# Stationary weights read with a step of two columns, and activations at another distance from the weights

## The chip, the cores and the metric

The kernel runs on one core of a Trainium2 chip. A core has a matrix engine (TensorE, PE in the rows; its weight loads are shown apart as PEld), VectorE (DVE), ScalarE (ACT), GpSimd (POOL) and SyncE (SP), which here only starts DMA transfers. All share an on-chip memory of 128 partitions (SBUF); TensorE writes to PSUM. The metric is the time of one execution on the device in microseconds (us), as the median over several runs. Before the change it is 2870.81 us over three runs (2864.52 to 2885.74).

## The reference

A transformer-like stack over 256 tokens of width 1024, batch 1, in float32. Six stages of the first block (two layers: feed-forward, a four-branch mixer, feed-forward) are followed by four layers of a second block (a mixer, cross-attention on a memory of 256 tokens, feed-forward). Nearly all the arithmetic is in products of the activations with weight matrices:

```
def _swiglu(x, w_gate, w_up, w_down):
    return (jax.nn.silu(x @ w_gate) * (x @ w_up)) @ w_down
...
for l in range(DEPTH):                                   # 2 layers
    x = x + 0.5 * _swiglu(_rmsnorm(x, ffn1_norm[l]), ffn1_w_gate[l], ffn1_w_up[l], ffn1_w_down[l])
    z = _rmsnorm(x, mix_norm[l]) @ w_in[l]               # 1024 x 6660, split over four branches
    ...                                                  # convolutions, two attentions
    x = x + merged @ w_out[l]
    x = x + 0.5 * _swiglu(_rmsnorm(x, ffn2_norm[l]), ffn2_w_gate[l], ffn2_w_up[l], ffn2_w_down[l])
for i in range(DEPTH_2):                                 # 4 layers
    x = x + mix                                          # diff_attention, hgrn2 or chunked_sgu
    x = x + mem_cross_attention(rmsnorm(x, norm_cross[i]), mem_n, ca_w_q[i], ca_w_kv[i], ca_w_o[i])
    x = x + swiglu(rmsnorm(x, norm_ffn[i]), ffn_w_gu[i], ffn_w_down[i])
return rmsnorm(x, norm_final)
```

D_FF is 2816 in both blocks.

## The kernel before

**Weight units.** The host cuts every weight matrix into units of 128 partitions x 2048 columns (1 MB). A column unit (`column_unit`) holds 256 output columns of a matrix with 1024 rows: eight blocks (k = 0 to 7) of 256 columns each. A row unit (`row_unit`) holds 256 rows of a matrix with 1024 columns: two blocks (kt) of 1024. `weight_units` lists some 460 of them in the order of use. They pass through a ring of five slots. SP starts the transfer of a unit into slot j of `raw` once TensorE has finished the unit that was there (semaphore `unit_done`, line 385). ScalarE copies it, rounded to float32r, into `wh` (`high`, line 1113), and GpSimd writes the remainder raw - wh, as float32r, into `wl` (`low`, line 400). `wl` lies on the same addresses as `raw`. TensorE waits for `low_ready`.

**Products.** Activations are split the same way into a high and a low part: ah and al, mh and ml, gh and gl (the gated values of the feed-forward stages), oh and ol, and others. `product` (lines 451 to 457) makes each block's product from three float32r matmuls, all accumulated into the same 256 columns of PSUM:

```
pe.matmul(out, sl, vh, ...)      # line 454
pe.matmul(out, sh, vl, ...)      # line 455
pe.matmul(out, sh, vh, ...)      # line 456
```

The second argument is stationary (128 columns, loaded into the array) and the third moves (256 columns). A unit is 16 such triples, 48 matmuls. In `features`, `features_by_input`, the two row-unit loops of `ffn` and the branch outputs of the mixer, the stationary operand is a run of 128 neighbouring columns of `wh` or `wl` (`wcut`), and activations move. In `tokens` and `tokens_by_input`, 128 tokens of the activations are stationary and 256 weight columns move. One unit of the four-branch mixer is used both ways: its first 128 columns by `features(..., fcs=1)`, and then by `tokens`.

**Order.** Every engine runs its own list of instructions in program order, and semaphores tie the lists together. Nothing is reordered by a scheduler.

**Addresses.** `sb` hands out SBUF space one tensor after another. `raw`/`wl` and `wh` (40,960 bytes per partition each) begin at 0 modulo 256, counted from `raw`. After `x` a gap of 192 bytes is left (line 147), so that ah, al, full, mh, ml, the parameters and constants begin at 192 modulo 256. A second gap (line 162) puts the work area with gh, gl, oh, ol and the rest at 192 too. Slots, blocks and halves of a block are multiples of 512 bytes apart. So in every product matmul the first byte of the activations is 192 behind the first byte of the weights, modulo 256. The constant matrices `decays` and the tensors lh and ll, which are multiplied with each other at lines 934 and 935, both begin at 192.

Of the kernel before, what the change touches and what calls it, by code (L numbers as in the profile page):

```python
# [25 lines left out]
P = 128  # L26
T = 256
TB = T // P
D = 1024
KD = D // P  # L30
DFF = 2816
FP = DFF // 256
UW = 2048
# [95 lines left out]
def build(nc, w_units, params_d, consts_d, hot_d, rel_d, x_d, mem_d, ws_d, bs_d, out_d,  # L129
          table_d, units=UNITS, stop_after=None):  # L130

    at = [nc.sbuf_base]
# [9 lines left out]
    raw_at = at[0]  # L142
    raw = sb("raw", RING * UW)
    wl = sb("wl", RING * UW, F32R, offset=at[0] - 4 * RING * UW)
    wh = sb("wh", RING * UW, F32R)
    x = sb("x", KD * T)
    at[0] += 192
    acts_at = at[0]
    ah = sb("ah", KD * T, F32R)
    al = sb("al", KD * T, F32R)  # L150
# [8 lines left out]
    root = sb("root", 4 * T + 8)  # L159
    rr = root[:, 3 * T:4 * T + 2]  # L160
    small = sb("small", 136)
    at[0] += (raw_at + 192 - at[0]) % 256
    work_at = at[0]
    WORK = 12288
    work = sb("work", WORK)
# [197 lines left out]
    with nc.Block() as block:  # L363
# [49 lines left out]
        def _(pe):  # L413
# [34 lines left out]
            def wcut(t, j, first, width):  # L448
                return t[:, j * UW + first:j * UW + first + width]

            def product(out, parts, start, stop, **kw):

                for k, (sh, sl, vh, vl) in enumerate(parts):
                    pe.matmul(out, sl, vh, start=start and k == 0, stop=False, **kw)  # L454
                    pe.matmul(out, sh, vl, start=False, stop=False, **kw)  # L455
                    ins = pe.matmul(out, sh, vh, start=False, stop=stop and k == len(parts) - 1, **kw)  # L456
                return ins

            def features(out, j, xh, xl, fcs=2, col=256, halfway=None):

                for fc in range(fcs):
                    if fc and halfway is not None:
                        halfway()
                    for k in range(KD):
                        parts = [(wcut(wh, j, k * 256 + fc * P, P), wcut(wl, j, k * 256 + fc * P, P),
                                  xh[:, k * T:(k + 1) * T], xl[:, k * T:(k + 1) * T])]
                        ins = product(out[:, fc * col:fc * col + T], parts, k == 0, k == KD - 1)
                return ins

            def features_by_input(out, j, xh, xl, acts, pieces=False):  # L470

                for k in range(KD):
                    if k % 2 == 0:
                        pe.wait_ge(acts, c.next(acts))
                    if k % 2 == 0 and pieces:
                        pe.wait_ge(*((low_ready, 1) if k == KD - 2 else (first_low_ready, k // 2 + 1)))
                    for fc in range(2):
                        parts = [(wcut(wh, j, k * 256 + fc * P, P), wcut(wl, j, k * 256 + fc * P, P),
                                  xh[:, k * T:(k + 1) * T], xl[:, k * T:(k + 1) * T])]
                        ins = product(out[:, fc * 256:fc * 256 + T], parts, k == 0 and fc == 0, k == KD - 1,  # L480
                                      skip_group_check=True)
                return ins
# [92 lines left out]
            def ffn(memory=False):  # L575
# [50 lines left out]
                def down(j, u, n, src, first, last):  # L626
                    pe.wait_ge(gated_ready, u + (r0 + 1))
                    pe.wait_ge(low_ready, n + 1)
                    for kt in range(2):
                        for dc in range(KD):  # L630
                            out = y[dc // 4][:, (dc % 4) * T:(dc % 4 + 1) * T]
                            parts = [(wcut(wh, j, kt * D + dc * P, P), wcut(wl, j, kt * D + dc * P, P),
                                      gh[:, src + kt * T:src + kt * T + T],
                                      gl[:, src + kt * T:src + kt * T + T])]
                            ins = product(out, parts, first and kt == 0 and dc % 2 == 0,
                                          last and kt == 1, skip_group_check=True)
                    ins.then_inc(unit_done, 1)
# [6 lines left out]
                for pair in range(KD // 2):  # L644
                    for u in (FP - 2, FP - 1):
                        j = (n1 + u) % RING
                        for dc in (2 * pair, 2 * pair + 1):
                            out = y[dc // 4][:, (dc % 4) * T:(dc % 4 + 1) * T]
                            parts = [(wcut(wh, j, kt * D + dc * P, P), wcut(wl, j, kt * D + dc * P, P),
                                      gh[:, u * 512 + kt * T:u * 512 + (kt + 1) * T],  # L650
                                      gl[:, u * 512 + kt * T:u * 512 + (kt + 1) * T]) for kt in range(2)]
                            ins = product(out, parts, False, u == FP - 1, skip_group_check=True)
                        if pair == KD // 2 - 1:
                            ins.then_inc(unit_done, 1)
                    if pair < KD // 2 - 1:
                        ins.then_inc(columns_done, 1)
# [59 lines left out]
            def mix1(l):  # L716
# [14 lines left out]
                keys, both = g_bank(copied), g_bank(copied)  # L731
                pe.wait_ge(low_ready, unit[0] + 1)
                j = unit[0] % RING
                features(keys, j, ah, al, fcs=1)
                tokens(both, j, ah, al).then_inc(unit_done, 1)
                unit[0] += 1
                projection(2, copied, ah, al)
# [2 lines left out]
                def branch_part(k):  # L740

                    b = BRANCHES[k // 5]
                    if PARTS[k % 5] == "gate":
                        projection(1, gate_used, ah, al)
                        return
                    outs = [s_bank(copied), s_bank(copied)]
                    for n in (2, 1):
                        also[sbank[0] - n] = (half_copied, c.next(half_copied))
                    pe.wait_ge(low_ready, unit[0] + 1)
                    j = unit[0] % RING  # L750
                    pe.wait_ge(acts_ready, c.next(acts_ready))
                    for dc in range(KD):
                        parts = [(wcut(wh, j, kt * D + dc * P, P), wcut(wl, j, kt * D + dc * P, P),
                                  bh[:, (2 * b + kt) * T:(2 * b + kt + 1) * T],
                                  bl[:, (2 * b + kt) * T:(2 * b + kt + 1) * T]) for kt in range(2)]
                        ins = product(outs[dc // 4][:, (dc % 4) * T:(dc % 4 + 1) * T], parts, True, True)
                    ins.then_inc(unit_done, 1)
                    unit[0] += 1
# [2011 lines left out]

def column_unit(a):

    return a.reshape(KD, P, 256).transpose(1, 0, 2).reshape(P, UW)


def row_unit(a):

    return a.reshape(2, P, D).transpose(1, 0, 2).reshape(P, UW)  # L2780


def columns_of(a):
    return [column_unit(a[:, n:n + 256]) for n in range(0, a.shape[1], 256)]


# [7 lines left out]
def weight_units(v):  # L2794
    out = []
    for l in range(L1):
        out += ffn_units(v["ffn1_w_gate"][l], v["ffn1_w_up"][l], v["ffn1_w_down"][l])
        win = v["w_in"][l]

        out += columns_of(win[:, 0:1280])  # L2800
        q = win[:, 1280:1536].reshape(D, 4, HD)[:, [0, 2, 1, 3]].reshape(D, 256)
        out += [column_unit(q)] + columns_of(win[:, 1536:2560])
        gates = win[:, 2564:]
        for b in BRANCHES:
            own = columns_of(gates[:, b * D:(b + 1) * D])
            name = ("conf_w_out", "sc_w_out", "swa_w_o", "fox_w_o")[b]
            out += own[0:2] + [row_unit(v[name][l])] + own[2:4]
        out += columns_of(v["w_out"][l])
        out += ffn_units(v["ffn2_w_gate"][l], v["ffn2_w_up"][l], v["ffn2_w_down"][l])
    for i, kind in enumerate(MIXERS):  # L2810
        kv = columns_of(v["ca_w_kv_2"][i])
        if kind == "diff":
            a = columns_of(v["da_w_in_2"][i // 3])
            out += [a[n] for n in (0, 4, 8, 9, 1, 5, 10, 11, 2, 6, 3, 7)] + kv[0:4]
            out += columns_of(v["da_w_out_2"][i // 3])
        elif kind == "hgrn":
            a = v["hg_w_in_2"][i // 3]
            out += (columns_of(a[:, D:2 * D]) + columns_of(a[:, 0:D]) + columns_of(a[:, 2 * D:]) + kv[0:4]
                    + columns_of(v["hg_w_out_2"][i // 3]))
        else:  # L2820
            a = v["sg_w_in_2"][i // 3]
            out += columns_of(a[:, D:]) + columns_of(a[:, 0:D]) + kv[0:4] + columns_of(v["sg_w_out_2"][i // 3])
        out += columns_of(v["ca_w_q_2"][i]) + kv[4:8] + columns_of(v["ca_w_o_2"][i])
        out += ffn_units(v["ffn_w_gu_2"][i][:, :DFF], v["ffn_w_gu_2"][i][:, DFF:], v["ffn_w_down_2"][i])
    assert len(out) == UNITS
    return np.stack(out)
# [74 lines left out]
```

## Time and profile before

| | |
|---|---|
| median of three runs | 2870.81 us |
| the profiled execution's own span | 2878.8 us |
| TensorE busy, matmuls | 2822.3 us (98%), 24,180 matmuls |
| TensorE busy, weight loads | 2771.7 us (96%) |
| GpSimd busy | 2108.9 us (73%) |
| ScalarE busy | 1333.4 us (46%) |
| VectorE busy | 1066.5 us (37%) |
| granted TensorE clock, mean | 0.989 |
| memory traffic | 496.88 MB, mean 173 GB/s |

The profile is of one execution. A matmul's record overlaps the next one's, since matmuls are pipelined and their ends are modelled: a record of about 280 ns does not mean that a matmul costs that much. What one costs in a stream is the distance from its start to the next one's start. In the groups of instructions, "G<-ah,wl 128\*128 128x256" names the output, then the moving operand, then the stationary one; 128x256 is the moving operand's shape.

### The profile page before, as it was taken

To read this page: it belongs to the slowest core of one execution; us is meant where nothing else is said; L and a number is where in the kernel's file an instruction comes from. 1 tells how busy PE (TensorE), PEld (TensorE's weight loads), DVE (VectorE), ACT (ScalarE), POOL (GpSimd) and SP (SyncE) were. 2 spreads that over 40 slices of the span, in tenths; PEclk is the share of its full clock that TensorE was granted. 3 is DMA by queue.
4 is the path that set the end of the run, shared out by engine and by line. 5 is a ranking of instruction groups with operands and counts; after the bars stand their busy time and mean duration, and the time that the engine had idled before them with its cause. 6 is when DMAs were issued, how large, how long until landed. Compare 5 with 4: busy or idle time off the path is not lost.

```text
span 2878.8 us, 55910 instructions
## 1 busy us (share of the span) xinstructions
PE 2822.3 (98%) x24180; PEld 2771.7 (96%) x24180; DVE 1066.5 (37%) x1865; ACT 1333.4 (46%) x1490; POOL 2108.9 (73%) x462
## 2 busy tenths in 40 slices
PE   8999999999999999999999999999999999999998
PEld 8999889999999899999999998999999999999998
DVE  4217534213155443445333144333123331453331
ACT  5335544344355454345443484444354443454442
POOL 6777657878876578776768783659886688767785
PEclk9999999999999899999999999999999999999999
DMA  7974344555554355554445542445554455544553
GB/s 231 193 198 170 135 144 176 191 185 188 199 184 152 112 192 189 182 185 147 168 169 191 191 177 87 158 144 197 191 204 153 147 195 196 191 147 161 176 192 116
DMA packets 74197, 496.88 MB, mean 173 GB/s; under 512 B 8399, under 2 KB 13135, under 8 KB 14968
## 3 DMA queue, kind: packets, MB, share of 16 engines
q1 hardware_dynamic: 68344, 485.88, 46.9%
q10 hardware_dynamic: 5632, 7.62, 2.7%
q8 instruction: 191, 3.13, 0.4%
q14 instruction: 30, 0.25, 0.0%
HBM read 490.05 MB, written 3.41 MB: 171 GB/s over the span
## 4 chain that ended last, share of the span: by engine, by line
PE 86%; POOL 4%; DMA 3%; issue 3%; DVE 2%; ACT 2%; ACTq 0%; SPq 0%; POOLq 0%; DVEq 0%
PE G L454 21%; PE G L456 21%; PE G L455 21%; PE S L454 5%; PE S L456 5%; PE S L455 5%; POOL wl L400 4%; DMA raw<-w_units 2%; PE G L691 1%; PE S L1042 1%; ACT wh L1113 1%; DMA bias<-tables 0%; PE S L842 0%; PE S L799 0%; PE S L805 0%
## 5 line engine op out<-in xcount | busy, mean ns | idle before, releaser
L400 POOL TENSOR_TENSOR wl<-raw,wh 128x2048 fp32r<-128x2048 f32 x458 | 2108.7, 4616 | 740.5 <-ACT wh L1113 719.0
L1113 ACT ACTIVATE wh<-raw 128x2048 fp32r<-128x2048 f32 x456 | 873.7, 1918 | 1045.6 <-DMA raw<-w_units 1045.5
L454 PE MATMUL G<-ah,wl 128*128 128x256 f32 x4304 | 1209.2, 281 | 15.6 <-DVE wl L1768 8.9
L455 PE MATMUL G<-al,wh 128*128 128x256 f32 x4304 | 1200.6, 279 | 0.0
L456 PE MATMUL G<-ah,wh 128*128 128x256 f32 x4304 | 1200.3, 279 | 0.0
L454 PEld LDWEIGHTS G<-ah,wl 128*128 128x128 f32 x4304 | 816.4, 190 | 24.1 <-issue 15.1
L455 PEld LDWEIGHTS G<-al,wh 128*128 128x128 f32 x4304 | 815.2, 189 | 0.6
L456 PEld LDWEIGHTS G<-ah,wh 128*128 128x128 f32 x4304 | 814.1, 189 | 0.0
L454 PE MATMUL S<-gh,wl 128*128 128x256 f32 x1408 | 391.4, 278 | 3.4 <-POOL wl L400 3.4
L455 PE MATMUL S<-gl,wh 128*128 128x256 f32 x1408 | 391.3, 278 | 0.0
L456 PE MATMUL S<-gh,wh 128*128 128x256 f32 x1408 | 391.2, 278 | 0.0
L454 PEld LDWEIGHTS S<-gh,wl 128*128 128x128 f32 x1408 | 265.0, 188 | 3.7 <-issue 3.7
L456 PEld LDWEIGHTS S<-gh,wh 128*128 128x128 f32 x1408 | 265.1, 188 | 0.0
L455 PEld LDWEIGHTS S<-gl,wh 128*128 128x128 f32 x1408 | 265.1, 188 | 0.0
L1921 DVE TENSOR_TENSOR G<-G,root 128x512 f32<-128x512 f32 x88 | 61.5, 698 | 361.3 <-PE G L456 361.3
L1959 DVE SCALAR_TENSOR_TENSOR S<-S,x 128x512 f32<-128x512 f32 x28 | 19.6, 700 | 367.1 <-PE S L456 365.9
L1919 DVE TENSOR_TENSOR G<-G,root 128x512 f32<-128x512 f32 x88 | 61.4, 698 | 184.4 <-PE G L456 184.1
L454 PE MATMUL G<-mh,wl 128*128 128x256 f32 x384 | 108.3, 282 | 3.3 <-DVE ml L2120 2.8
L454 PE MATMUL G<-wh,al 128*128 128x256 f32 x384 | 108.0, 281 | 0.8 <-DVE ll L2563 0.8
L455 PE MATMUL G<-wl,ah 128*128 128x256 f32 x384 | 107.2, 279 | 0.0
L456 PE MATMUL G<-wh,ah 128*128 128x256 f32 x384 | 107.1, 279 | 0.0
L456 PE MATMUL G<-mh,wh 128*128 128x256 f32 x384 | 106.9, 279 | 0.0
(371 smaller groups left out, 3786.3 us busy)
## 6 DMA issues: line engine op xcount, KB each, us to landing
raw<-w_units SPq DMA_DIRECT2D x459, 1024.0 KB, 4.8
bias<-tables ACTq DMA_DIRECT2D x24, 128.0 KB, 3.2
tables<-trow ACTq DMA_DIRECT2D x12, 192.0 KB, 9.0
con<-consts SPq DMA_DIRECT2D x1, 1056.0 KB, 16.8
x<-x_in SPq DMA_DIRECT2D x4, 256.0 KB, 5.8
raw<-w_units SPq DMA_DIRECT2D x4, 256.0 KB, 6.9
memx<-mem_in ACTq DMA_DIRECT2D x1, 1024.0 KB, 7.4
out<-full SPq DMA_DIRECT2D x4, 256.0 KB, 2.5
```

What stands on the lines that cost most here:

```text
L400: pool.tensor_tensor(wl[:, j * UW:(j + 1) * UW], raw[:, j * UW:(j + 1) * UW], wh[:, j * UW:(j + 1) * UW].bitcast(F32), ALU.subtract)\
L454: pe.matmul(out, sl, vh, start=start and k == 0, stop=False, **kw)
L455: pe.matmul(out, sh, vl, start=False, stop=False, **kw)
L456: ins = pe.matmul(out, sh, vh, start=False, stop=stop and k == len(parts) - 1, **kw)
L691: ins = pe.matmul(out, v_of(kc), pt[:, kc * 512 + n * P:kc * 512 + (n + 1) * P], start=kc == 0, stop=kc == nk // P - 1)
L1042: ins = pe.matmul(out[:, h * T:(h + 1) * T], qf[:, f * T + g * P:f * T + (g + 1) * P], kc[:, f * T:(f + 1) * T], start=dc == 0, stop=dc == 1)
L1113: act.activation(wh[:, j * UW:(j + 1) * UW], raw[:, j * UW:(j + 1) * UW], ACT.Copy)\
L1919: dve.tensor_tensor(pairs(gate), pairs(gate), along, ALU.mult).then_inc(scaled, 1)
L1921: dve.tensor_tensor(pairs(value), pairs(value), along, ALU.mult).then_inc(up_scaled, 1)
L1959: dve.scalar_tensor_tensor(xs if last else held[k], held[k], factor, xs, ALU.mult, ALU.add)\
```

## The change

It has two parts. First, wherever weights are stationary, the 128 columns of a load are every other column of a run of 256 (`every_other`: the even ones for the first half of the outputs, the odd ones for the second). The host interleaves the two halves of every 256 columns beforehand (`interleaved`), so that the same numbers reach the same outputs. Units whose weights move (`token_columns_of`) are left in the old order, and so is the unit that is used both ways, whose 128 columns are still read with a step of one (`first_features`). Second, both gaps are 96 bytes instead of 192: activations, constants and work area begin 96 behind the weights modulo 256. `decays` and lh still begin at the same place modulo 256.

```diff
@@ addresses @@
-    at[0] += 192
+    at[0] += 96
     acts_at = at[0]
...
-    at[0] += (raw_at + 192 - at[0]) % 256
+    at[0] += (raw_at + 96 - at[0]) % 256
@@ TensorE @@
+            def every_other(j, first, odd):
+
+                return tuple(wcut(t, j, first, 2 * P).rearrange("p (i f) -> p f i", f=2)[:, odd, :] for t in (wh, wl))
...
-            def features(out, j, xh, xl, fcs=2, col=256, halfway=None):
-
-                for fc in range(fcs):
+            def features(out, j, xh, xl, halfway=None):
+
+                for fc in range(2):
                     if fc and halfway is not None:
                         halfway()
                     for k in range(KD):
-                        parts = [(wcut(wh, j, k * 256 + fc * P, P), wcut(wl, j, k * 256 + fc * P, P),
-                                  xh[:, k * T:(k + 1) * T], xl[:, k * T:(k + 1) * T])]
-                        ins = product(out[:, fc * col:fc * col + T], parts, k == 0, k == KD - 1)
+                        parts = [(*every_other(j, k * 256, fc), xh[:, k * T:(k + 1) * T], xl[:, k * T:(k + 1) * T])]
+                        ins = product(out[:, fc * 256:fc * 256 + T], parts, k == 0, k == KD - 1)
                 return ins
+
+            def first_features(out, j, xh, xl):
+
+                for k in range(KD):
+                    parts = [(wcut(wh, j, k * 256, P), wcut(wl, j, k * 256, P),
+                              xh[:, k * T:(k + 1) * T], xl[:, k * T:(k + 1) * T])]
+                    product(out[:, 0:T], parts, k == 0, k == KD - 1)
...
@@ row units: both loops of ffn, and the mixer's branch outputs @@
-                            parts = [(wcut(wh, j, kt * D + dc * P, P), wcut(wl, j, kt * D + dc * P, P),
+                            parts = [(*every_other(j, kt * D + dc // 2 * 256, dc % 2),
@@ host @@
+def interleaved(a):
+
+    return a.reshape(a.shape[0], -1, 2, P).transpose(0, 1, 3, 2).reshape(a.shape)
...
 def row_unit(a):
 
-    return a.reshape(2, P, D).transpose(1, 0, 2).reshape(P, UW)
+    return interleaved(a).reshape(2, P, D).transpose(1, 0, 2).reshape(P, UW)
 
 
 def columns_of(a):
+    return [column_unit(interleaved(a[:, n:n + 256])) for n in range(0, a.shape[1], 256)]
+
+
+def token_columns_of(a):
     return [column_unit(a[:, n:n + 256]) for n in range(0, a.shape[1], 256)]
```

`features_by_input` is edited as `features` is. The order of the instructions on every engine and their waits are the same before and after; only source lines are numbered differently.

## Rows read from the trace of the kernel before

**Rows 1.** The page's busy times with instruction counts; the core's span and clock.
```profile
PE 2822.3 (98%) x24180; PEld 2771.7 (96%) x24180; DVE 1066.5 (37%) x1865; ACT 1333.4 (46%) x1490; POOL 2108.9 (73%) x462
...
core 0: 2878.8 us, clock 0.989
```

**Rows 2.** TensorE's groups by form, line 454: count | busy us, mean ns | idle before.
```profile
L454 PE MATMUL G<-ah,wl 128*128 128x256 f32 x4304 | 1209.2, 281 | 15.6 <-DVE wl L1768 8.9 <-DVE wl L1800 3.4 <-DVE merged L2178 3.2
...
L454 PE MATMUL S<-gh,wl 128*128 128x256 f32 x1408 | 391.4, 278 | 3.4 <-POOL wl L400 3.4
...
L454 PE MATMUL G<-mh,wl 128*128 128x256 f32 x384 | 108.3, 282 | 3.3 <-DVE ml L2120 2.8 <-DVE logf L2655 0.5
L454 PE MATMUL G<-wh,al 128*128 128x256 f32 x384 | 108.0, 281 | 0.8 <-DVE ll L2563 0.8
...
L454 PE MATMUL G<-oh,wl 128*128 128x256 f32 x384 | 106.5, 277 | 0.0
...
L454 PE MATMUL G<-wh,ml 128*128 128x256 f32 x256 | 72.2, 282 | 0.0
...
L454 PE MATMUL S<-mh,wl 128*128 128x256 f32 x128 | 35.9, 280 | 1.5 <-issue 1.5
...
L454 PE MATMUL G<-soh,wl 128*128 128x256 f32 x64 | 19.5, 304 | 4.2 <-ACT kc L1238 4.2
...
L454 PE MATMUL G<-hoh,wl 128*128 128x256 f32 x64 | 17.8, 278 | 0.0
```

**Rows 3.** TensorE by stretch: window, its us, busy (matmuls), clock, DMA share, GB/s.
```profile
42.00:177.00 135.00, 135.00 (x1148) 1.00 0.91 202
467.00:641.00 174.00, 174.00 (x1480) 1.00 0.51 181
655.00:827.00 172.00, 172.00 (x1520) 1.00 0.54 192
...
1148.00:1254.00 106.00, 106.00 (x903) 1.00 0.52 184
1486.00:1653.00 167.00, 167.00 (x1476) 1.00 0.54 193
...
1942.00:2114.00 172.00, 172.00 (x1520) 1.00 0.55 197
2308.00:2473.00 165.00, 165.00 (x1458) 1.00 0.54 192
2704.00:2864.00 160.00, 160.00 (x1414) 1.00 0.48 171
```

**Rows 4.** Matmuls of 128 moving columns: timeline, chain (start, us), and group by form.
```profile
1354.58 1.47 PE L702 MATMUL G<-con,full 128*128 128x128 f32 x12
...
1438.83 7.15 PE G L691 x64
...
L702 PE MATMUL G<-con,full 128*128 128x128 f32 x48 | 6.2, 272 | 0.0
```

**Rows 5.** Timeline of TensorE (start, us): `decays` products, and first and last of twenty token matmuls.
```profile
1733.85 0.28 PE L454 MATMUL G<-wh,al 128*128 128x256 f32 x1
...
1736.09 0.28 PE L455 MATMUL G<-wl,ah 128*128 128x256 f32 x1
...
1743.76 0.28 PE L935 MATMUL S<-decays,ll 128*128 128x256 f32 x1
...
1744.48 0.28 PE L935 MATMUL S<-decays,ll 128*128 128x256 f32 x1
```

**Rows 6.** The chain that ended last: shares of the span by engine and line.
```profile
PE 86%; POOL 4%; DMA 3%; issue 3%; DVE 2%; ACT 2%; ACTq 0%; SPq 0%; POOLq 0%; DVEq 0%
PE G L454 21%; PE G L456 21%; PE G L455 21%; PE S L454 5%; PE S L456 5%; PE S L455 5%; POOL wl L400 4%; DMA raw<-w_units 2%; PE G L691 1%; PE S L1042 1%; ACT wh L1113 1%; DMA bias<-tables 0%; PE S L842 0%; PE S L799 0%; PE S L805 0%
```

**Rows 7.** The low split's group (count | busy, mean ns | idle before), and the weights' transfers.
```profile
L400 POOL TENSOR_TENSOR wl<-raw,wh 128x2048 fp32r<-128x2048 f32 x458 | 2108.7, 4616 | 740.5 <-ACT wh L1113 719.0
...
raw<-w_units SPq DMA_DIRECT2D x459, 1024.0 KB, 4.8
```

More of the change, by code:

```diff
@@ L477, in features_by_input @@
                     for fc in range(2):
-                        parts = [(wcut(wh, j, k * 256 + fc * P, P), wcut(wl, j, k * 256 + fc * P, P),
-                                  xh[:, k * T:(k + 1) * T], xl[:, k * T:(k + 1) * T])]
+                        parts = [(*every_other(j, k * 256, fc), xh[:, k * T:(k + 1) * T], xl[:, k * T:(k + 1) * T])]
                         ins = product(out[:, fc * 256:fc * 256 + T], parts, k == 0 and fc == 0, k == KD - 1,
@@ L648, in ffn @@
                             out = y[dc // 4][:, (dc % 4) * T:(dc % 4 + 1) * T]
-                            parts = [(wcut(wh, j, kt * D + dc * P, P), wcut(wl, j, kt * D + dc * P, P),
+                            parts = [(*every_other(j, kt * D + dc // 2 * 256, dc % 2),
                                       gh[:, u * 512 + kt * T:u * 512 + (kt + 1) * T],
@@ L733, in mix1 @@
                 j = unit[0] % RING
-                features(keys, j, ah, al, fcs=1)
+                first_features(keys, j, ah, al)
                 tokens(both, j, ah, al).then_inc(unit_done, 1)
@@ L752, in branch_part @@
                     for dc in range(KD):
-                        parts = [(wcut(wh, j, kt * D + dc * P, P), wcut(wl, j, kt * D + dc * P, P),
+                        parts = [(*every_other(j, kt * D + dc // 2 * 256, dc % 2),
                                   bh[:, (2 * b + kt) * T:(2 * b + kt + 1) * T],
@@ L2801, in weight_units @@
         q = win[:, 1280:1536].reshape(D, 4, HD)[:, [0, 2, 1, 3]].reshape(D, 256)
-        out += [column_unit(q)] + columns_of(win[:, 1536:2560])
+        out += [column_unit(interleaved(q))] + token_columns_of(win[:, 1536:1792])
+        out += columns_of(win[:, 1792:2304]) + token_columns_of(win[:, 2304:2560])
         gates = win[:, 2564:]
@@ L2810, in weight_units @@
     for i, kind in enumerate(MIXERS):
-        kv = columns_of(v["ca_w_kv_2"][i])
+        keys, values = v["ca_w_kv_2"][i][:, 0:D], v["ca_w_kv_2"][i][:, D:]
+        kv = columns_of(keys) + token_columns_of(values)
         if kind == "diff":
-            a = columns_of(v["da_w_in_2"][i // 3])
+            a = v["da_w_in_2"][i // 3]
+            a = columns_of(a[:, 0:2 * D]) + token_columns_of(a[:, 2 * D:])
             out += [a[n] for n in (0, 4, 8, 9, 1, 5, 10, 11, 2, 6, 3, 7)] + kv[0:4]
@@ L2817, in weight_units @@
             a = v["hg_w_in_2"][i // 3]
-            out += (columns_of(a[:, D:2 * D]) + columns_of(a[:, 0:D]) + columns_of(a[:, 2 * D:]) + kv[0:4]
+            out += (columns_of(a[:, D:2 * D]) + columns_of(a[:, 0:D]) + token_columns_of(a[:, 2 * D:]) + kv[0:4]
                     + columns_of(v["hg_w_out_2"][i // 3]))
@@ L2821, in weight_units @@
             a = v["sg_w_in_2"][i // 3]
-            out += columns_of(a[:, D:]) + columns_of(a[:, 0:D]) + kv[0:4] + columns_of(v["sg_w_out_2"][i // 3])
+            out += token_columns_of(a[:, D:]) + columns_of(a[:, 0:D]) + kv[0:4] + columns_of(v["sg_w_out_2"][i // 3])
         out += columns_of(v["ca_w_q_2"][i]) + kv[4:8] + columns_of(v["ca_w_o_2"][i])
```

## The prediction
> **What bounds the kernel now.** I read the page's busy times first: the reader is to see TensorE busy for 98% of the span, no other engine over 73%, and a granted clock of 0.989 [rows 1]. TensorE's waits are small: the worst group is preceded by 15.6 us of idle time, most of the others by 0 to 4 us [rows 2]. So the time is the number of matmuls times their pitch (start to start), and only a change of pitch can move it much.
>
> The number comes from the groups by form [rows 2]. In a name like G<-ah,wl the moving operand stands first and the stationary one second. The seven groups of line 454 with wl as stationary operand hold 4304 + 1408 + 384 + 384 + 128 + 64 + 64 = 6736 matmuls, and lines 455 and 456 have one each beside every one of them: 20,208. The two groups with wh moving (token units) have 384 + 256 = 640, so 1920 with their partners. The mixer's one unit with `fcs=1` runs twice, 48 matmuls, and keeps step one. That leaves **20,160 matmuls whose load changes**, 1920 token matmuls with only their distance changed, and about 2,050 others.
>
> The pitch comes from the table of long unbroken stretches [rows 3]. A matmul's record is some 0.28 us long, so a window counts 2.4 more than fit in it. 467 to 641 us: 174.00 / (1480 - 2.4) = **117.8 ns**. 655 to 827 us: 172.00 / (1520 - 2.4) = **113.3 ns**. Every row of the table gives one or the other, nothing between, at a granted clock of 1.00 (2.4 GHz) and at a DMA share of 0.91 as of 0.51. So this is not memory traffic, nor the clock, nor waiting: the same instructions with the same operands run in one of two locked rhythms. The rows at 117.8 add up to 415 us (3,524 matmuls), those at 113.3 to 836 us (7,376), a mean of 1251 / 10,900 = **114.8 ns**.
>
> What else the array does at that clock is the yardstick [rows 4]. Twelve transposes, 128 moving columns each, take 1.47 us with the last one's 0.27 in it: (1.47 - 0.27) / 11 = **109 ns**. Sixty-four matmuls of 128 moving columns take 7.15 us on the chain: **111.7 ns**. In both, moving and stationary operand are 128 columns of 4 bytes, 512 bytes each per pitch. In the product matmuls the moving operand has 1024 bytes and the stationary one 512.
>
> **The change, part by part.** (1) *Step of two.* The 128 columns of a load now lie across 1024 bytes, so the weight stream walks over as many bytes in a pitch as the moving stream. Addresses of both, modulo 256, then keep their distance; before, with one stream walking twice as fast, the distance went round. My mechanism is that the 4 to 9 ns above 109 are what the two reads cost each other where they pass. The rows in which both streams walk equally fast, 109 and 111.7 ns, are the nearest ones for the price. I take their middle, 110.4 ns, and keep both ends. No row shows a strided load. 20,160 x (114.8 - 110.4) = 89 us; the ends are 20,160 x 5.8 = 117 and 20,160 x 3.1 = 62 us.
>
> (2) *Distance 96 for 192.* One place shows that distance counts with step one [rows 5]. `decays` and lh both begin 192 behind the weights, a distance of 0 from each other: the last six pitches take 1744.48 - 1743.76 = 0.72 us, 120.0 ns, which is neither of the product's rhythms. Nothing shows 96. For step two the distance is constant and not 0, so I cost it at nothing beyond (1). For the 1920 token matmuls (stationary ah, moving wh, both step one) it is open: they run at 117.9 ns in the rows shown (1736.09 - 1733.85 over 19 pitches) and elsewhere at 113.3; at worst all go to 120 and at best to 113.3. From 115.6, the middle of the two rhythms, that is +8 or -4 us. I take 0.
>
> (3) *Everything else.* The host's interleaving is outside the time. Instruction order and waits are the same on every engine; the number of bytes fetched from memory too. `first_features` reads the same operands as before.
>
> **What of it lies on the path.** The chain that ended last has 3 x 21% + 3 x 5% = 78% of the span in the product lines [rows 6], 2245 us, while all product matmuls take 22,128 x 114.8 = 2540 us and more. So 0.87 to 0.88 of them lie on it; the rest runs beside POOL, DMA and the mixers' steps. TensorE is busy there too, so the true share is between 0.88 and 1. I take 0.93: 89 x 0.93 = 83 us. Ends: 62 x 0.88 = 54 and 117 x 1 = 117 us.
>
> Does another engine take over? A unit is 48 matmuls, 5.51 us now at the mean and 5.30 us at 110.4. The low split on POOL takes 4.62 us a unit, and the weights land 4.8 us after issue, with four units' lead [rows 7]. Both still fit, at 87% and 91% of a unit. At 109 ns (5.23 us) they fit too. What is late next is the ends of stages, where the ring is drained: POOL stands on the chain for 4%, DMA for 3% [rows 6], and those stretches do not shrink.
>
> The sum goes against the profiled execution: 2878.8 - 83 = **2796 us**. Its span is 8 us above the median of the three runs (2870.8). The two rhythms explain such differences: all product matmuls at 113.3 or at 117.8 are 22,128 x 4.5 ns = 98 us apart, so a fifth of them in the other rhythm makes the 21 us between lowest and highest run. Where no rhythm is left to choose, the runs should stand closer, and I move nothing for the median. The forecast's own range is 2762 to 2825 us.
>
> **What the skill would say.** The Trainium skill (TensorE: Matmul & The Clock Gate, Part 2) says that the engine has two independent SBUF read ports and that loading the next weights takes no bandwidth from the running matmul; SBUF — State Buffer (Who interferes with whom) adds that TensorE waits on nobody. By that rule neither edit changes anything. The same TensorE page gives, under Back-to-back issue gap, N/2.4 + 2.5 ns for an isolated gap, 109 ns at 256 columns; this trace's 113.3 and 117.8 do not fit that, while the transposes' 109 ns does for the same total time. It would be 2879 us by the rule and 2796 by the rows.
>
> **The rivals.**
> *The bytes touched are what costs (slower), 0.16.* With 512 + 512 bytes walked over in a pitch the row says 109 to 111.7 ns, with 1024 + 512 it says 113.3 to 117.8. Another 512 bytes may cost another 4.3 to 6.1 ns, 119 to 121 ns in all: 20,160 x 4.3 to 6.1 = 87 to 123 us more, 2966 to 3002 us. For it: the trace fits a price per byte as well as a price for passing. Against it: 120 ns at distance 0 with the same bytes, and two rhythms with the same bytes. It decides as soon as the pitch is over 116.2 ns (1% of 2870 us over 20,160).
> *The strided load is itself slower, 0.08.* If the reader fetches bytes at the old rate, a load of 1024 bytes takes twice 109 ns and becomes the pitch: 20,160 x 103 ns = 2080 us more, 4960 us. It decides once a load needs over 115 ns. No row shows such a load. The Trainium skill (SBUF — State Buffer, Door 1: The DMA port swizzle) says that SBUF has lines of 16 bytes, that full bandwidth needs at least two hits on each, and that every move to a new line costs something: a step of two gives exactly two hits and twice the moves. No trace here shows it.
> *The rhythms stay, in another mix, 0.13.* The streams are still started by the same two queues, and the lock could be one of starts, not addresses. All product matmuls at 113.3 would give 20,160 x 1.5 = 30 us less, 2849 us; the old mix gives 2879. Against it: the lock survives for hundreds of us, which asks for something periodic in the operands, and all addresses here repeat modulo 256.
> *Nothing happens, 0.08.* The ports' rule above, as a mechanism: the reads never meet, and the 4 to 9 ns come from the array. Then 2871 to 2879 us.
> *The forecast, 0.55*: 2762 to 2825 us.
>
> **How the numbers follow.** A measurement of this kernel can tell about 1% from no change, 29 us, since its own runs spread by 0.7%. Faster by over 1% (under 2842 us): the forecast's 0.55 and 0.05 of the changed mix, 0.60. Within 1%: the other 0.08 of the mix, 0.08 of nothing, and 0.01 of the bytes, 0.17. Slower: 0.15 + 0.08 = 0.23. The predicted time is the forecast's. The range must hold the forecast, the mix and nothing (0.76), and a quarter of the bytes' case, if only part of its price is paid: 2750 to 2950 us.
>
> **What would show it.** *Step right:* unbroken stretches with one pitch of 109 to 112 ns, at the same granted clock; matmul records shorter than the mean of 278 to 281 ns now [rows 2], nearer the 272 ns of the transposes [rows 4]. *Mechanism wrong:* pitches of 113.3 and 117.8 again. *Bytes:* one pitch near 120. *Load:* a weight-load record that grows, and TensorE idle before matmuls of line 454. *Cover gone:* idle on TensorE released by POOL's line 400 beyond a few us. *Token matmuls:* their pitch tells the distance's own price.

## The result, and the profile after

The changed kernel is slower: 2974.64 us (median of 4 runs, 2973.45 to 2980.99) against 2871.57 us, a ratio of 1.036 (95% interval 1.033 to 1.040). The profiled execution has a span of 2979.1 us against 2878.8, 100.3 us more. The forecast was 2796 us, faster, with a range up to 2950.

The busy shares lie within two points of those before and the clock is the same [rows 1], with the same number of instructions on every engine. These are the page's busy times and the core's line of the kernel after:

```profile
PE 2928.3 (98%) x24180; PEld 2878.9 (97%) x24180; DVE 1062.0 (36%) x1865; ACT 1333.3 (45%) x1490; POOL 2103.7 (71%) x462
...
core 0: 2979.1 us, clock 0.989
```

The waits did not move either. These are the first two groups of product matmuls by form, after (count | busy us, mean ns | idle before), to be read beside the first two of [rows 2]: idle is 14.7 and 4.5 us where it was 15.6 and 3.4, and a matmul's record grew from 281 and 278 ns to 286 and 284:

```profile
L458 PE MATMUL G<-ah,wl 128*128 128x256 f32 x4304 | 1232.4, 286 | 14.7 <-DVE wl L1777 8.9 <-DVE wl L1809 3.4 <-DVE merged L2187 2.5
L458 PE MATMUL S<-gh,wl 128*128 128x256 f32 x1408 | 399.9, 284 | 4.5 <-POOL wl L400 4.5
```

The time is in the pitch. This is TensorE by stretch, after (window, its us, busy (matmuls), clock, DMA share, GB/s), to be read as [rows 3]:

```profile
480.00:640.00 160.00, 160.00 (x1336) 1.00 0.51 181
700.00:820.00 120.00, 120.00 (x1002) 1.00 0.52 182
1530.00:1690.00 160.00, 160.00 (x1336) 1.00 0.52 185
2030.00:2150.00 120.00, 120.00 (x1003) 1.00 0.51 184
```

160.00 / (1336 - 2.4) = 120.0 ns, in all four, and the clock is still 1.00. The two rhythms of 113.3 and 117.8 ns are gone; there is one, whose matmuls come 115 to 125 ns apart in a repeating pattern with a mean of 120.0. Summed from start to start, the 20,208 matmuls with stationary weights take 2468.7 us against 2367.4. These 101.3 us are the whole of the difference of 100.3 between the spans; token matmuls (230.3 against 230.2 us) and everything else (260.7 against 261.7) stayed.

### The profile page after: what moved, and what is told of

Its sections match the earlier page's. It is cut to its first block, busy times and chain, and to the rows that moved or that the text cites. A ratio compares the mean times of both kernels' runs of the same rounds, so it can differ in the third digit from the quotient of the medians.

```text
span 2979.1 us, 55910 instructions
## 1 busy us (share of the span) xinstructions
PE 2928.3 (98%) x24180; PEld 2878.9 (97%) x24180; DVE 1062.0 (36%) x1865; ACT 1333.3 (45%) x1490; POOL 2103.7 (71%) x462
## 4 chain that ended last, share of the span: by engine, by line
PE 88%; POOL 3%; DMA 3%; issue 3%; DVE 2%; ACT 2%; SPq 0%; ACTq 0%; POOLq 0%; DVEq 0%
PE G L458 21%; PE G L460 21%; PE G L459 21%; PE S L458 6%; PE S L460 6%; PE S L459 6%; POOL wl L400 3%; DMA raw<-w_units 2%; PE G L700 1%; PE S L1051 1%; ACT wh L1122 1%; PE S L851 0%; DMA bias<-tables 0%; PE S L808 0%; PE S L814 0%
## 5 line engine op out<-in xcount | busy, mean ns | idle before, releaser
L458 PE MATMUL G<-ah,wl 128*128 128x256 f32 x4304 | 1232.4, 286 | 14.7 <-DVE wl L1777 8.9
L460 PE MATMUL G<-ah,wh 128*128 128x256 f32 x4304 | 1223.7, 284 | 0.0
L459 PE MATMUL G<-al,wh 128*128 128x256 f32 x4304 | 1223.7, 284 | 0.0
L458 PEld LDWEIGHTS G<-ah,wl 128*128 128x128 f32 x4304 | 858.3, 199 | 23.2 <-issue 14.8
L459 PEld LDWEIGHTS G<-al,wh 128*128 128x128 f32 x4304 | 858.3, 199 | 0.5
L460 PEld LDWEIGHTS G<-ah,wh 128*128 128x128 f32 x4304 | 858.0, 199 | 0.0
L458 PEld LDWEIGHTS S<-gh,wl 128*128 128x128 f32 x1408 | 280.2, 199 | 4.6 <-issue 4.6
L459 PEld LDWEIGHTS S<-gl,wh 128*128 128x128 f32 x1408 | 280.3, 199 | 0.0
L458 PE MATMUL G<-oh,wl 128*128 128x256 f32 x384 | 109.2, 284 | 0.0
L459 PE MATMUL G<-ol,wh 128*128 128x256 f32 x384 | 108.8, 283 | 0.0
## 6 DMA issues: line engine op xcount, KB each, us to landing
tables<-trow ACTq DMA_DIRECT2D x12, 192.0 KB, 9.1
```

## The experiments

**Theories.** A: the addresses of the two operands set the rhythm, so step and distance act together. S: a load of step two is slower by itself, wherever the operands lie. D: distance 96 is bad, whatever the step. Names of the runs: e for variants of the kernel, m for tables measured with TensorE alone.

### Each part alone

e1 is the kernel before with the change's distance; e2 is the kernel after with 192 in the same two lines. The edit of e1:

```diff
-    at[0] += 192
+    at[0] += 96
-    at[0] += (raw_at + 192 - at[0]) % 256
+    at[0] += (raw_at + 96 - at[0]) % 256
```

> Only the distance is changed, 192 to 96; the loads keep a step of one. If the distance alone is to blame (theory D), the time is that of the change, about 2975 us, with product pitches at 120 ns. If the step alone is to blame (theory S, the bytes touched), it is that of before, 2865 to 2886 us, with stretches at 113.3 and 117.8 ns. If the two act together through addresses (theory A), it is neither in full: some other pitch, between 109 and 120 ns.

Measured: 2977.7 us, ratio 1.034 (1.031 to 1.038) to the kernel before.

> Only the step is changed, one to two; activations stay 192 behind the weights. Theory S expects the time of the change, about 2975 us and one pitch of 120 ns. Theory D expects the time of before. Theory A expects another pitch: with streams that walk equally fast the distance should matter much, so 192 gives something clearly apart from 120 ns, on either side.

Measured: 2972.4 us, ratio 1.033 (1.029 to 1.036). Stretches of e1, to be read as above:

```profile
480.00:640.00 160.00, 160.00 (x1336) 1.00 0.52 185
700.00:820.00 120.00, 120.00 (x1003) 1.00 0.52 185
```

and of e2:

```profile
480.00:640.00 160.00, 160.00 (x1336) 1.00 0.51 183
700.00:820.00 120.00, 120.00 (x1003) 1.00 0.52 183
```

Both have 120.0 ns, as both parts together have. Each part alone costs the whole 3.3 to 3.4%, and the second adds next to nothing. Neither S nor D alone says that; there are two ways to 120 ns, and the pitch does not tell which.

The weight loads' own records do tell. These are the loads of the largest group (count | busy us, mean ns | idle before): before, e1, after, e2.

```profile
L454 PEld LDWEIGHTS G<-ah,wl 128*128 128x128 f32 x4304 | 816.4, 190 | 24.1 <-issue 15.1 <-DVE merged L2178 4.4 <-DVE wl L1800 3.6
L454 PEld LDWEIGHTS G<-ah,wl 128*128 128x128 f32 x4304 | 818.0, 190 | 22.6 <-issue 14.0 <-DVE merged L2178 3.7 <-DVE wl L1800 2.6
L458 PEld LDWEIGHTS G<-ah,wl 128*128 128x128 f32 x4304 | 858.3, 199 | 23.2 <-issue 14.8 <-DVE merged L2187 3.7 <-DVE wl L1809 3.6
L458 PEld LDWEIGHTS G<-ah,wl 128*128 128x128 f32 x4304 | 843.4, 196 | 22.7 <-issue 13.8 <-DVE merged L2187 3.7 <-DVE wl L1809 3.0
```

In e1 the pitch went to 120.0 ns and the load's record stayed at 190 ns. With step two it grew to 196 and 199 ns, which is the sign that the prediction had named for a slower load.

### A table of pitches

m1 is no model. TensorE multiplies resident operands in the pattern of the kernel's triples, 192 matmuls per setting, with nothing beside it:

```
weights_still(step, d): for each unit, half, k: product(out, wh/wl with step, activations d bytes behind)
settings: step 1 with d = 0, 16 .. 240; step 2 the same; step 4 with 0, 96, 192; activations stationary; odd widths
```

> Not the model: TensorE alone multiplies resident operands, in the pattern of the product matmuls (triples, 16 to a unit, four units or 192 matmuls per setting), and nothing else runs. Settings in this order, then the same in reverse: step one with distances 0, 16, ... 240; step two with the same sixteen; step four with 0, 96, 192; activations stationary with 0, 32, ... 224; then 96 each of matmuls with 512 moving columns, with 64 stationary columns, with 128 moving columns, and plain float32. The output is not the reference's. Theory S expects two flat rows: 113 to 118 ns for step one at every distance, 120 ns for step two at every distance, more for step four. Theory D expects the same curve over the distance for steps one and two. Theory A expects the distance to matter, differently for step one and step two, and a distance at which step two reaches 109 to 112 ns. If the rhythms come from starts and not from addresses, the same setting gives different pitches in its two passes.

Distance matters with step one: 113.3 ns at 112 and 192 in both passes and at 64 in one of the two, 120.0 at 0, 80 and 96, the rest 116.7 to 119.3 (240 gave 117.1 in one pass and 120.0 in the other). With step two it matters little: 117.8 at 80, 118.3 at 16, elsewhere 119 to 121; nothing near 109 to 112. These are windows of m1 (columns as above): step one at 192 and at 208, and step four at 0:

```profile
302.00:320.00 18.00, 18.00 (x161) 1.00 0.00 1
325.00:342.00 17.00, 17.00 (x145) 1.00 0.00 1
765.00:800.00 35.00, 35.00 (x151) 1.00 0.00 0
```

The first is 18.00 / (161 - 2.4) = 113.5 ns, the second 17.00 / (145 - 2.4) = 119.2, and step four takes 233 ns at a clock of 1.00, twice as long. TensorE alone, with no other engine at work, shows the kernel's pitches of 113.3, 117.8 and 120.0 ns.

### What limits a pitch

m2 takes the pair apart: finer distances, both operands moved together, narrow loads, other numbers of moving columns (96 matmuls each, in two orders).

```
run(w, a, still, moving, mstep): matmul(out[0:still, 0:moving], weights[w/4 : +still], activations[a/4 : +moving])
```

> Not the model, output not the reference's: TensorE alone, 96 matmuls per setting, float32r, step one, the whole list forward and then backward. Settings: moving operand 0, 4, ... 252 bytes behind the weights; weights and activations moved together with 192 between them (16 places); weights moved alone with activations in place (16); together with 112 between them (8); 8, 16, 32, 64 and 96 stationary columns with the activations at 0, 48, 112, 192; 64 to 512 moving columns at 0, 112, 192; the moving operand with a step of two at five distances; the weights moved by further 256 to 2048 bytes. If the distance between the two operands decides (theory A), moving both together changes nothing, and moving the weights alone gives the mirrored curve. If the moving operand's own place decides, moving both together changes the pitch and moving the weights alone does not. If it is the two reads that cost each other (the prediction's mechanism), a load of 8 columns leaves 109 ns at every distance; if the excess belongs to the moving stream or the array, it stays at 113 to 120 ns.

Two windows of m2, with a load of **8 columns** instead of 128, at distances 48 and 112:

```profile
1219.00:1227.00 8.00, 8.00 (x73) 1.00 0.00 0
1231.00:1238.00 7.00, 7.00 (x64) 1.00 0.00 0
```

8.00 / (73 - 2.4) = 113.3 ns. With loads of 8, 16 and 32 columns, 21 of the 24 measurements gave 113.3, at four distances; with 64 and 96 columns the excess was back (113.3 to 119.0, and 116.0 to 118.7). **113.3 ns is the floor of 256 moving float32r columns**, with hardly a load beside them; 512 columns took 226.7 at best, and 256 columns read with a step of two 226.7 to 235.6. So the 109 ns that the prediction took as reachable are not. Of 4 to 9 ns of excess, 4 never could go.

In this list the place of the pair does not matter: with 192 or 112 between them, both moved together over 256 bytes, all 48 measurements gave 113.3. This list proves less than it seems. Its settings follow each other without a pause, and with fresh starts (m3 and m4 below) distance 192 gave 113.3 in only seven of twelve with the weights at 0, and in four of six at 32. So a rhythm once entered seems to outlive a change of place at the same distance. Distances that are not multiples of 16 gave 116.9 to 123.3 ns, never 113.3.

### Does the distance decide, or the start?

e3 takes the best distance of m1 into the kernel, with step one. Since tensors begin at multiples of 32, the weights were moved by 16 and the activations placed at 128. e4 does the same for step two with 80. `wl` and `wh` are moved as `raw` is, and the work area is placed as the activations are.

```diff
-    raw = sb("raw", RING * UW)
+    raw = sb("raw", RING * UW + 64)[:, 4:4 + RING * UW]
...
-    at[0] += 192
+    at[0] += (raw_at + 128 - at[0]) % 256
```

> Step one as before, activations 112 instead of 192 bytes behind the weights. In the first table distance 112 gave 113.3 ns in both passes with step one, as 192 did, while 64 gave 113.3 in one and 117.8 in the other. Theory A (addresses set the rhythm) expects product pitches of 113.3 ns: if in all stretches, some 2880 - 30 = 2850 us and runs close together; if 112 too has two rhythms, 2840 to 2890. A theory by which the distance is only good or bad by its size (96 bad, so its neighbour 112 bad) expects 2970 us and 120 ns.

Measured: 2969.4 us, ratio 1.034 (1.032 to 1.037). The expectation of 2850 fell.

> Step two as in the change, activations 80 behind the weights, the distance at which the first table gave step two its lowest pitch in both passes beside 16: 117.8 ns against 120. If the table holds in the kernel, 20,160 x 2.2 ns = 44 us less than the change, 2930 us. If the table says nothing about the kernel, 2975 us.

Measured: 3018.0 us, ratio 1.051 (1.048 to 1.054): slower than the change, where 2930 was expected. Two stretches of e3, then two of e4:

```profile
480.00:640.00 160.00, 160.00 (x1373) 1.00 0.53 186
1530.00:1690.00 160.00, 160.00 (x1336) 1.00 0.50 179
```

```profile
480.00:640.00 160.00, 160.00 (x1312) 1.00 0.50 178
700.00:820.00 120.00, 120.00 (x984) 1.00 0.50 177
```

e3 has 116.7 ns (160.00 / (1373 - 2.4)) in one stretch and 120.0 in another, e4 122.2. So the tables had missed something. m3 looks for it in the start: 60 matmuls per setting, each begun twelve times after different waits and different matmuls. It also loads with other steps while few columns move.

> Not the model, output not the reference's. TensorE alone, float32r. For each of sixteen distances, 60 matmuls (128 stationary columns, 256 moving) are begun twelve times: eight times after a wait for ScalarE of varied length, four times after two matmuls of another width; first with loads of step one, then of step two. Behind that 160 and 192 moving columns with load steps one to four, and loads of 8 to 96 columns with step two. If the pitch belongs to the distance (as the tables seemed to say), all twelve starts of a distance agree. If the distance only offers several rhythms and the start picks one (which the 120 ns of the kernel at distance 112 speak for), they differ: distance 112 should then show 113.3 and 120 ns. If a load of step two costs nothing by itself, 160 and 192 moving columns stay at 111.7 ns with it; if it is what made 120 ns, they rise to 115 to 120.

The lowest and highest of twelve starts, in ns, over the last 36 matmuls of each, by distance:

```
distance       0     16     32     48     64     80     96    112    128    144    160    176    192    208    224    240
step one    120.0  116.6  116.6  118.3  113.3  118.2  119.9  113.3  118.7  116.6  117.3  119.1  113.3  116.6  118.2  117.1
        to  120.0  118.7  117.8  118.4  117.8  120.1  120.1  113.3  120.0  118.7  118.7  119.3  117.8  119.4  118.5  117.1
step two    120.0  118.3  120.0  120.0  120.0  117.8  120.0  119.9  120.0  120.0  120.0  119.0  119.9  119.9  119.9  119.9
        to  120.0  118.4  121.0  120.0  121.7  117.8  120.0  120.2  121.2  120.1  120.8  119.1  120.1  120.1  120.1  120.1
```

At 192 seven starts gave 113.3 and five 117.8: the kernel's two rhythms [rows 3], chosen by the start. At 112 all twelve gave 113.3, so the start does not explain e3.

And the load. Windows of m3 with **160 moving columns**, too few to be the limit: two of step one, then two of step two:

```profile
2958.00:2967.00 9.00, 9.00 (x83) 1.00 0.01 2
2968.50:2978.50 10.00, 10.00 (x92) 1.00 0.00 0
3001.00:3011.00 10.00, 10.00 (x87) 1.00 0.01 2
3012.00:3022.00 10.00, 10.00 (x87) 1.00 0.00 0
```

Step one: 10.00 / (92 - 2.4) = 111.6 ns, the same at four distances, and 111.6 to 111.7 with 128, 192 and 224 moving columns too (m2, m3). Step two: 10.00 / (87 - 2.4) = 118.2 ns, 117.7 to 120.0 over the eight measurements with 160 or 192 moving columns. **Where the moving columns are too few to be the limit, step two costs 6 to 8 ns more than step one**, and the pitch is then above the 113.3 of 256 moving columns. S holds, for step two. The load's records agree: over the sixteen distances with 256 moving columns their means are 187.5 to 192.0 ns with step one, whether the pitch is 113.3 or 120.0, and 193.0 to 198.3 ns with step two.

How much of it is the load alone is not separated. The pitch of step two varies with the distance and is higher with 192 moving columns (118.3 to 120.0) than with 160 (117.7 to 118.3), so the moving operand's read seems to have a part in it. And under 256 moving columns a step-two load of only 64 columns still gave 115.5 to 120.0 ns.

m3 also has steps three and four. These are one window of step three with 192 moving columns and one of step four with 160, at half the clock:

```profile
3312.00:3321.00 9.00, 9.00 (x54) 1.00 0.01 2
3125.00:3146.00 21.00, 21.00 (x92) 0.50 0.00 1
```

Step three takes 173 to 175 ns at a clock of 1.00, step four 233 to 240 ns at 0.50, and m1 had 233 to 237 for step four at 1.00. A step-one load goes with the clock (213.3 ns at 0.50 in m2, 111.7 at 1.00); a step-four load does not.

### The weights' own place

The two runs that missed both had the weights at 16 modulo 256. In m2, with the weights moved alone, places 16 modulo 32 had often left the curve: distance 112 gave 118.3 and 116.7 ns with the weights at 144. e5 therefore leaves the weights at 0 and moves all activations to 112, by four columns inside tensors that begin at 96; e6 is the changed kernel with activations at 80 in the same way (al, full, mh, ml and the work area go with ah); m4 repeats m3 with the weights at 16, six starts each.

```diff
-    at[0] += 192
+    at[0] += (raw_at + 96 - at[0]) % 256
...
+    def later(name, width, dt=F32):
+        at[0] += 4 * width
+        return sb(name, width + 8, dt, offset=at[0] - 4 * width)[:, 4:4 + width]
...
+    ah = later("ah", KD * T, F32R)
```

> Step one, weights left at 0 modulo 256 and all activations moved to 112 (in the run before this, the weights were moved to 16 and the activations to 128). In the third table, with weights at 0, distance 112 gave 113.3 ns from all twelve starts. If the distance and the weights' own place modulo 32 both count (what rows with weights at odd multiples of 16 hint at), the kernel now runs its product matmuls at 113.3 ns throughout: 2880 less some 30 us, about 2845 us, and the runs lie close together. If the kernel differs from the tables for another reason (other engines' traffic), it stays at 2970 us.

Measured: 2857.7 us (12 runs, 2852.5 to 2865.6), ratio **0.995** (0.993 to 0.997): half a percent faster than the kernel before. Its profiled span is 2856.2 us, 22.6 less than that of before. Three stretches of e5:

```profile
700.00:820.00 120.00, 120.00 (x1047) 1.00 0.56 199
1530.00:1690.00 160.00, 160.00 (x1402) 1.00 0.54 191
2700.00:2840.00 140.00, 140.00 (x1238) 1.00 0.47 166
```

The last is 140.00 / (1238 - 2.4) = 113.3 ns, and of 348 uninterrupted runs of 48 product matmuls 306 take 5.44 us, 48 times 113.3 (in the kernel before 213 of 348, with 116 at 117.8). The other 42 are each the first behind a pause, at up to 115.0 ns, where the rhythm is not reached yet. (The other two windows come to 114.9 and 114.3 ns, with short pauses and other matmuls in them.) The expected 2845 us was too low for two reasons: token matmuls take 235.4 us where they took 230.2, and the product matmuls gained 26.6 us, not 30.

> Step two with the weights at 0 and the activations at 80. The third table gave 117.8 ns there from all twelve starts, against 120 ns at 96. If tables with weights at 0 carry over, 20,160 x 2.2 ns = 44 us less than the change, about 2930 us: the best that step two reached at any of sixteen distances, and still slower than the kernel before. With the weights at 16 it had been 3018 us.

Measured: 2938.0 us, ratio 1.023 (1.019 to 1.027), for an expected 2930: units of 5.653 us or 117.8 ns, as the table had said. In the profiled executions the product matmuls take 43 us less than in the change, as expected, and the token matmuls 4 us more. It is the best of step two, and still slower than before.

> Not the model, output not the reference's. As the third table, but with the weights moved to 16 bytes and the activations with them (sixteen distances, six starts each, steps one and two); then activations stationary and weights moving at sixteen distances; then eight pairs of weight place and distance; then loads of step one and two with 160 moving columns at weight places 4, 8, 16. If only the distance counts, weights at 16 repeat the third table, with 113.3 ns at 112 and 117.8 at 80 for step two. If the weights' place modulo 32 counts, distance 112 gives 116.7 to 120 ns and step two at 80 gives 122.2, what the two kernels with moved weights showed, while places 32, 64 and 128 give 113.3 at 112.

With the weights at 16, distance 112 gave 120.0 ns from five starts and 118.3 from one; e3 has most of its units at 120.0 and some at 118.3, and its 116.7 of the first window showed only in m2, with the weights at 144. Step two at 80 gave 122.2 to 122.3, which is e4. Distance 192 gave 113.3 from all six starts, where weights at 0 had given it from seven of twelve, and weights at 32 from four of six (the expectation of e7 below counts one less in each). With the weights at 32, 64 and 128, distance 112 was 113.3 again. At 4 and 8 bytes both distances cost 120.1 to 123.7. So the pair of distance (modulo 256) and place decides, and for some pairs the start. That the place counts modulo 32 fits these places, and the list of m2 with the weights moved alone; only the distances 112 and 192 were tried at several places with fresh starts. With activations stationary at 112 m4 gave 120.0 ns from all starts, and at 192 117.7 to 117.8. With 160 moving columns, 111.7 ns with step one and 117.7 to 120.0 with step two, at places 4, 8 and 16 too.

e7 puts the new cell of the table to use, with step one: weights at 16 as in e3, and activations at 208, by four columns inside tensors that begin at 192, as in e5.

```diff
+    raw = sb("raw", RING * UW + 64)[:, 4:4 + RING * UW]
...
+    at[0] += (raw_at + 192 - at[0]) % 256
```

> Step one, weights at 16 and activations at 208 modulo 256: the distance of the kernel before, 192, with the weights' place moved by 16. The fourth table gave 113.3 ns from all six starts there (3 of 6 with the weights at 32, 6 of 12 with them at 0). Product matmuls should run at 113.3 ns throughout, as with weights at 0 and activations at 112. Token matmuls should run at 118.4 ns (the same table with the roles exchanged: stationary at 16 modulo 32, distance 64) against 120 there, 1920 x 1.6 ns = 3 us less: about 2855 us, 0.5 to 0.6% under before, with close runs. If the table's rhythm does not carry over, a mix as before, 2865 to 2885 us.

Measured: 2855.9 us (6 runs, 2853.6 to 2857.0), ratio **0.993** (0.991 to 0.996), for an expected 2855. This is less than both kernels take, by 0.7% for the one before. The runs lie within 3.4 us of each other where before's 11 beside them lie within 19. Against e5 it is 2 us faster, which is the size expected from the token matmuls (233.4 us against 235.4 in the profiled executions) but within the spread.

## Why the prediction was wrong, point by point

- **The bound was right.** TensorE's pitch decides; waits, clock and other engines played no part. The 101.3 us of the product matmuls are 20,208 times 5.0 ns. The path factor of 0.93 was too low: 20,160 times the 5.2 ns from 114.8 to 120.0 are 105 us, and nearly all of them reached the span.
- **The failing step is the price of part (1).** "The rows in which both streams walk equally fast, 109 and 111.7 ns, are the nearest ones for the price." They do not measure that. The term was -4.4 ns a matmul (114.8 to 110.4), -89 us; it measured +5.2 ns (114.8 to 120.0), +101 us. The 111.7 ns [rows 4] are those of a 128-column load that nothing longer covers: m3 has 111.6 to 111.7 with 160 moving columns of float32r. These rows are not float32r at all: `pt2` and `vc` are plain float32, and the 64 records belong to 32 matmuls of the program, two for each (in m1, 96 plain float32 matmuls left 192 records). The 109 ns are transposes of 128 columns, another kind of operation, so that they meet a figure for 256 columns says nothing. For float32r the floor is 113.3 ns at 256 columns (m2). The yardstick mixed kinds of matmul, and the floor was above both ends (109 and 111.7) of the pitch that the forecast used.
- **The gain that was there was at most 1.5 ns.** From a mean of 114.8 to 113.3, and e5 and e7 took it, with step one.
- **The mechanism was half right.** The excess over 113.3 ns depends on the distance between the two operands (m3, e1, e5 and e7) and mostly goes with loads of 8 to 32 columns (m2), so it belongs to the two reads together. That they cost each other where they pass is an inference from this. That equal speeds would end it was wrong. Step two has 117.8 to 121.7 ns over all sixteen distances.
- **Part (2), distance at nothing, was wrong**, though the sign stood in [rows 5]. e1 shows +3.4% for 96 alone. It could be seen that distance 0 made 120 ns; that 96 does so too could not. With step two in place it adds almost nothing: e2, at 192, is at 120.0 ns as well.
- **The rival of the slower strided load was right in kind.** It named its point of decision, "once a load needs over 115 ns", and the load needs 117.7 to 120 (m3), with a longer record. Its price was far off: a doubling, 218 ns, which only step four reaches (233). It took the pitch of a 512-byte load as the speed at which bytes are read; but in [rows 3] the moving operand's 1024 bytes pass in 113.3 ns, so the bound for a load across 1024 bytes was near there, and the case deserved far more than 0.08.
- **The rival of the bytes gave the right number for the wrong reason.** It said 119 to 121 ns and 2966 to 3002 us. But e1 touches no more bytes than before and has 120.0 ns, and e6 touches all of them and has 117.8. As a price per byte it fell.
- **The ports' rule** (the Trainium skill, TensorE: Matmul & The Clock Gate, Part 2, and SBUF — State Buffer, Who interferes with whom) says that the load takes nothing from the running matmul and that TensorE waits on nobody. The trace disagrees: with the same instructions and the weights in place, the distance between the operands alone moved the pitch from 113.3 ns (112) to 120.0 (96) in m3. **The lines' rule** (SBUF — State Buffer, Door 1: The DMA port swizzle) asks for two hits on each line of 16 bytes and puts a price on every move to a new line. Two hits were not enough here: a step-two load took 117.7 to 120 ns for 111.7, and 256 moving columns with step two 226.7 to 235.6 for 113.3 and up. A price for the moves fits the direction of both.
- **The two rhythms as the cause of the spread between runs** are supported, not shown, since only one execution of the kernel before has a trace. e5 and e7, with one rhythm for the products, spread less than before does beside them (13 us against 30, and 3 against 19). The 13 us of e5 have some other cause.

What stays open: why step two costs 6 to 8 ns, and what in the memory repeats every 256 and 32 bytes. No run here looks inside. One reading fits the numbers without being shown: reads go by the bytes that they walk over. The moving operand takes 113.3 ns for 1024 bytes and 226.7 at best for 2048, whether as 512 columns or with a step of two; a load takes 173 to 175 ns for 1536 bytes (step three) and 233 for 2048 (step four, at either clock). An estimate from these, 57 to 58 ns per 512 bytes, gives 113 to 117 ns for a load of step two; the measured 117.7 to 120 lie above it. Nor was it tried whether a row of the table holds for operands of 2 bytes.

## What to carry to other kernels

A yardstick must be of the same kind of instruction: before a row is used as the price of a change, say what limits that row. Where matmuls follow each other without waits and the pitch is above the floor of the moving columns, the addresses of the two operands are a free setting worth a table: one run of TensorE alone, some thirty settings with several starts each, predicted the kernel's pitch in e5, e6 and e7. The table must have the kernel's own places: m1, with the weights elsewhere than in e3 and e4, missed them by 4% and 3%. Keep float32r loads at step one.

## What the runs showed of the hardware that was not expected

- 256 moving float32r columns take 113.3 ns at a granted clock of 1.00 (2.4 GHz) even with an 8-column load; a 128-column load takes 111.7 ns; with step two 117.7 to 120, step three 173 to 175, step four 233. At a granted clock of 0.50 a step-one load takes 213.3 ns, and a step-four load still 233 to 240.
- A stream of equal matmuls falls into a rhythm with an exact mean (113.33, 116.67, 117.78, 118.33, 120.00 ns), and in the kernel keeps it until a pause: the longest unbroken stretch of the kernel before lasts 183 us at 117.8 ns. Behind the pause it may take another.
- With step one the rhythm depends on the distance of the operands modulo 256 and on the weights' place, as far as tried modulo 32. Best here: distance 112 with the weights at 0 (12 of 12 starts at 113.3), or 192 with the weights at 16 (6 of 6). Worst: 123.7 ns with the weights at 8 and distance 112, and 123.3 with them at 16 and distance 208 (two starts of six). Distances off multiples of 16 bytes never gave 113.3.
- Traffic of other engines does not show in it: the kernel, with DMA at half of its time, has the same rhythms as TensorE alone.
